# A hybrid HGRN2 / S5 / mixture-of-experts decoder step on one core: small matrix products laid side by side in the array, token columns split into equal halves, and the HGRN2 chunks issued ahead of their state

## What is computed

```
ada = silu(c) @ w_ada + b_ada             # 9 conditioning rows, 6 vectors of 1024 (+ 2 of w_ada_final)
proj = adanorm(x) @ w_in                  # q, f, i, g, u of 512 columns each
HGRN2 (4 heads, chunks of 32):  o = mask(q k) v + q S ;  S = decay * S + k v    # chunk after chunk
S5 (32 groups of 16 inputs, 64 complex states):  y = scan(u) ; y = glu(gelu(y))
x = x + gate1 * ([o | y] @ w_out)
x = x + gate2 * moe(adanorm(x))           # 4 groups x 8 experts, top 2 of the best group
y = adanorm_final(x)
```

## Time and profile before

| | us |
|---|---|
| runs shown (three) | 1017.25, 1021.3, 1029.67 |
| median | 1021.3 |
| the profiled execution | 1030.67 |
| its span, first to last instruction | 1028.7 |

### The profile page before, as it was taken

How to read it: one execution, slowest core, us unless ns; L and a number is a source line. 1 busy time by engine, 2 the same in 40 slices (tenths; PEclk the granted TensorE clock), 3 DMA queues, 4 the chain that set the end, 5 groups by cost and what they waited for, 6 DMA issues and landing times.

```text
span 1028.7 us, 8565 instructions
## 1 busy us (share of the span) xinstructions
PE 809.2 (79%) x3102; PEld 392.5 (38%) x3102; DVE 353.7 (34%) x905; ACT 208.3 (20%) x445; POOL 87.5 (9%) x134
## 2 busy tenths in 40 slices
PE   6189999999997999899679999934967787788800
PEld 1025566653353443777544442211422232233300
DVE  2029373546733234322523534340110101110157
ACT  2042123333344452100002101200110100110122
POOL 1000101120100001000001000032110101110040
PEclk9687999999998999555679999966988988898955
DMA  7940202024440106300159414553999999999552
GB/s 265 342 143 36 72 11 82 1 83 164 162 165 7 41 0 218 70 0 1 52 180 347 123 41 149 229 177 90 349 392 416 401 366 415 392 394 385 237 193 92
DMA packets 62844, 187.24 MB, mean 182 GB/s; under 512 B 12475, under 2 KB 17723, under 8 KB 50518
## 3 DMA queue, kind: packets, MB, share of 16 engines
q1 hardware_dynamic: 39542, 154.46, 39.5%
q10 hardware_dynamic: 16256, 17.04, 5.6%
q0 software_dynamic: 7008, 15.25, 4.6%
HBM read 176.84 MB, written 17.22 MB: 189 GB/s over the span
## 4 chain that ended last, share of the span: by engine, by line
PE 64%; DMA 15%; DVE 6%; ACTq 5%; issue 4%; ACT 3%; SPq 1%; POOL 1%; POOLq 0%; DVEq 0%
PE ps L1543 60%; DMA sb<-in_moe_w_up 12%; DVE sb L939 3%; PE ps L1595 2%; ACTq L613 2%; SPq L348 1%; ACTq L607 1%; PE ps L1690 1%; POOL token_of_row L507 1%; ACT sb L708 1%; DVE sb L1524 1%; DVE sb L1536 1%; DMA token_of_row<-sb 1%; DMA sb<-in_b_ada_final 1%; DMA sb<-y_rows,sb 1%
## 5 line engine op out<-in xcount | busy, mean ns | idle before, releaser
L1543 PE MATMUL ps<-sb 128*64 128x512 f32 (+10 forms) x2718 | 755.7, 508 | 106.5 <-DMA sb<-in_moe_w_up 51.3
L1543 PEld LDWEIGHTS ps<-sb 128*128 128x128 f32 (+4 forms) x2718 | 344.3, 174 | 485.7 <-issue 423.5
L939 DVE TENSOR_TENSOR sb<-sb 128x16 f32<-128x16 f32 (+18 forms) x368 | 162.6, 482 | 101.8 <-ACT sb L708 47.9
L939 DVE TENSOR_TENSOR sb<-ps,sb 128x256 f32<-128x256 f32 (+6 forms) x69 | 29.0, 441 | 238.3 <-ACT sb L885 188.4
L1595 PE MATMUL ps<-sb 128*128 128x128 f32 (+1 forms) x208 | 31.6, 302 | 35.4 <-DMA sb<-h_rows,sb 31.8
L1595 PEld LDWEIGHTS ps<-sb 128*128 128x128 f32 (+1 forms) x208 | 27.1, 197 | 52.4 <-DMA sb<-h_rows,sb 31.9
L885 ACT ACTIVATE sb<-ps 128x256 f32<-128x256 f32 x16 | 6.2, 385 | 177.0 <-PE ps L1543 177.0
L1246 DVE SCALAR_TENSOR_TENSOR sb<-sb,ps 128x128 f32<-128x128 f32 x60 | 16.8, 343 | 44.8 <-PE ps L1543 44.8
L515 POOL DMA_INDIRECT sb<-h_rows,sb x16 | 16.3, 1021 | 152.9 <-PE ps L1595 150.4
L708 ACT COPY sb<-ps 32x144 f32<-32x144 f32 x64 | 26.2, 410 | 11.1 <-PE ps L1543 9.6
L655 ACT ACTIVATE sb<-ps 128x512 f32<-128x512 f32 x12 | 7.2, 597 | 101.8 <-PE ps L1543 101.8
(11 more groups left out here) (229 smaller groups left out, 348.2 us busy)
## 6 DMA issues: line engine op xcount, KB each, us to landing
sb<-in_moe_w_gate SPq DMA_DIRECT2D x32, 1024.0 KB, 13.7
sb<-in_moe_w_up SPq DMA_DIRECT2D x32, 1024.0 KB, 16.1
sb<-in_moe_w_down SPq DMA_DIRECT2D x32, 1024.0 KB, 9.0
sb<-in_w_ada SPq DMA_DIRECT2D x12, 2048.0 KB, 8.8
sb<-in_w_in SPq DMA_DIRECT2D x5, 2048.0 KB, 9.3
sb<-in_w_ada_final SPq DMA_DIRECT2D x4, 2048.0 KB, 14.2
sb<-in_w_out SPq DMA_DIRECT2D x2, 2048.0 KB, 7.7
sb<-in_x_prompt SPq DMA_DIRECT2D x4, 512.0 KB, 10.9
```

The source lines that it names most:

```text
L939: return dve.tensor_tensor(out, x0, x1, op)
L1543: return pe.matmul(out, lhsT, rhs, start=start, stop=stop, skip_group_check=True)
```

## The change

1. Conditioning: the eight products of a piece go to four column groups of the array (PSUM partitions 0, 32, 64, 96; two products each, nine rows). ACT copies 105 rows of the bank to `part`, whose last rows hold the biases, and one product with a 0/1 matrix `pick` adds the four parts and the bias. For the first four pieces eight small products with `part` as the stationary side give columns at once, so that `ada_col` and its transposes go. A piece's bank is free for the piece after the next when its sum has been copied out.
2. The 576 columns are split 288 + 288 in `proj_cols`, the GLU and its sum of squares.
3. HGRN2: U products are issued for two chunks at a time, alternating between two row groups, into four banks, ahead of the state; the output products of a tile come after three of its four states, alternating between the four column groups; the transposes of a tile come one tile later; `Sr` has 8 buffers, in slot 0. On DVE the norm of a tile follows the state chain of the next one.
4. S5: the eight Toeplitz products go to four column groups of bank 6; ACT copies two of the four pairs, DVE the other two (8 copies each).

The core of the diff:

```
+        part = at(PART, 512)
+        pick = v2(take(16 * C9), 16, C9)
-        Sr = [v2(EXT + 2560 + 512 * k, H, P) for k in range(3)]
+        NSR = 8
+        Sr = [v2(512 * k, H, P) for k in range(NSR)]
+        ubank = [ps[6], ps[7], ps[0], ps[1]]
...
             # POOL
+            pool.memset(part, 0.0)
+            step(pool.memset(pick, 0.0))
+            for g in range(4):
+                step(pool.affine_select(out=pick, ...
...
             # ACT
+            def ada_parts(n):
+                act.wait_ge(S["ada_part"], n + 1)
+                if n >= 1:
+                    act.wait_ge(S["ada_sum"], n)
+                act.copy(part[0:PROWS, :], ada_bank(n)[0:PROWS, :]).then_inc(S["ada_pb"], 1)
...
+            for n_ in range(4):
+                ada_cols(n_)
+                if n_ + 1 < 4:
+                    ada_parts(n_ + 1)
...
-                        act.copy(Tm[32 * s:32 * s + 32, 2 * hf:2 * hf + 2, 32 * s:],
-                                 ps[6 + hf][0:32, :].rearrange("p (q n) -> p q n", q=2)[:, :, 0:w]).then_inc(S["s5_Tout"], 1)
+                        act.copy(Tm[32 * s:32 * s + 32, q, 32 * s:], ps[6][32 * q:32 * q + 32, 0:2 * P - 32 * s])\
+                            .then_inc(S["s5_Tout"], 1)
...
             # DVE
+                dve.wait_ge(S["s5_T"], 4 * (r + 1))
+                for q in (2, 3):
+                    for s in range(4):
+                        ins = dve.tensor_copy(Tm[32 * s:32 * s + 32, q, 32 * s:], ps[6][32 * q:32 * q + 32, 0:2 * P - 32 * s])
...
+            for t in range(PT):
+                state_chain(t)
+                if t >= 1:
+                    norm_o(t - 1)
                 if t + 1 < PT:
                     mask(t + 1)
-                norm_o(t)
+            norm_o(PT - 1)
...
             # PE
-                for c in range(KC):
-                    ins = mm(bank[q:q + C9, :], cT[:, c, :], w[:, c, :], c == 0, False)
-                j = 2 * v + h
-                mm(bank[q:q + C9, :], ident[0:16, j:j + 1].to_broadcast([16, C9]), bias16, False, True).then_inc(S["ada_mm"], 1)
+                if n >= 2:
+                    pe.wait_ge(S["ada_out"], n - 1)
+                for c in range(KC):
+                    g = 32 * (c % 4)
+                    ins = mm(bank[g:g + C9, :], cT[:, c, :], w[:, c, :], c < 4, c >= 4)
+                ins.then_inc(S["ada_part"], 1)
...
+                pe.wait_ge(S["ada_pb"], n + 1)
+                mm(ada_bank(n)[q:q + C9, :], pick[:, 2 * v + h, :], part, True, True).then_inc(S["ada_sum"], 1)
...
-                    mm(b0[:, :], lhs, hT[:, c, 0:TP], c == 0, c == KC - 1)
-                    ins = mm(b1[:, 0:NS], lhs, hT[:, c, TP:NT], c == 0, c == KC - 1)
+                    mm(b0[:, 0:NH], lhs, hT[:, c, 0:NH], c == 0, c == KC - 1)
+                    ins = mm(b1[:, 0:NH], lhs, hT[:, c, NH:NT], c == 0, c == KC - 1)
...
+                for k in range(2):
+                    for q in range(4):
+                        ins = mm(ps[6][32 * q:32 * q + 32, 0:256], AB[k][:, q, L - 1, :],
+                                 CA[k][:, q, 0:L, :].rearrange("p j h -> p (j h)"), k == 0, k == 1)
...
+            def chunk_pair(p):
+                if p >= 2:
+                    pe.wait_ge(S["s_upd"], 2 * (p - 1))
+                for h in range(H):
+                    hs = slice(P * h, P * (h + 1))
+                    for c in (2 * p, 2 * p + 1):
+                        js = slice(32 * (c % 4), 32 * (c % 4) + 32)
+                        ins = mm(ubank[c % 4][:, hs], KhT[js, c // 4, hs], V[js, c // 4, hs], True, True)
+                ins.then_inc(S["u_mm"], 1)
```

More of the change, by code:

```diff
@@ L168, in decoder_step @@
         iota_i = at(take(E), E)
+        yix, xix = (at(take(NU), NU) for _ in range(2))
+        roff = at(take(E), E)
         cb2 = v2(take(TILES * E), TILES, E)
@@ L299, in used_up @@
             if n < 4:
-                return S["ada_mm"], 2 + n + 1
+                return S["ada_part"], n + 1
             if n < 7:
@@ L849, in _ @@
                                     accum_out=RT["gs"][:, t:t + 1]))
-            for v, h in ADA_ROUTER[2:]:
-                late_row(v, h)
+            ada_parts(14)
+            ada_rows(14)
+            ada_parts(15)
+            ada_rows(15)
             act.wait_ge(S["rt_exp"], 2)
@@ L1233, in norm_o, with state_chain @@
                 ins.then_inc(S["o_norm"], 1)
-            mask(0)
-            for t in range(PT):
+            def state_chain(t):
                 for j in range(4):
                     c = 4 * t + j
-                    dve.wait_ge(S["u_mm"], c + 1)
-                    new, old, U = Sr[(c + 1) % 3], Sr[c % 3], ps[6 + c % 2].rearrange("p (h v) -> p h v", h=H)
+                    dve.wait_ge(S["u_mm"], c // 2 + 1)
+                    if j == 3 and t >= 1:
+                        dve.wait_ge(S["o_mm"], t)
+                    new, old, U = Sr[(c + 1) % NSR], Sr[c % NSR], ubank[c % 4].rearrange("p (h v) -> p h v", h=H)
                     if c == 0:
@@ new lines, in _, with ada_bank, ada_parts @@
+            pe.wait_ge(S["bc_out"], 1)
+            def ada_bank(n):
+                return ps[(2 if n >= 12 else 0) + n % 2]
+            def ada_parts(n):
+                bank, w = ada_bank(n), next_piece()
+                if n == 1:
+                    pe.wait_ge(S["bc_out"], 2)
+                if n >= 2:
[4 more added lines that the diff above has]
+                ins.then_inc(S["ada_part"], 1)
@@ L1673, in beside_s5 @@
                 for w in beside[j]:
-                    ada_row(*w) if j >= 4 else proj_cols(w)
+                    if j < 4:
+                        proj_cols(w)
+                        continue
+                    ada_parts(w)
+                    if w > 4:
+                        ada_sum_rows(w - 1)
             pe.wait_ge(S["const"], 1)
@@ L1751, in scores, with turn_out @@
                 ins.then_inc(S["sc_mm"], 1)
+            def chunk_pair(p):
[7 more added lines that the diff above has]
+                ins.then_inc(S["u_mm"], 1)
+            def turn_out(t):
+                r = ROWS[t]
+                pe.wait_ge(S["o_norm"], t + 1)
+                if t >= 1:
+                    pe.wait_ge(S["mix_out"], t)
+                for h in range(H):
+                    ins = pe.transpose(ps[3][:, P * h:P * h + r], mtok[t % 2][0:r, P * h:P * (h + 1)], ident[0:r, 0:r])
+                ins.then_inc(S["mix_tr"], 1)
             scores(0)
```

291 lines of the change are left out of this document (141 added, 150 removed).

## The result

The changed kernel takes 947.93 us (median of four runs, 945.03 to 951.06) against 1021.65 us before (four runs, 1017.25 to 1029.67): 0.927 of the time, 95% interval 0.921 to 0.934. The forecast was 930 us, the range 902 to 962. The profiled execution took 951.06 us.

What follows compares the result with a forecast made beforehand. The prediction took PE to bound the chain for 64% of the span and DMA, in the experts, for 15%. Its terms summed to 92.5 us off 1030.67, giving 938.2, scaled by 0.9% to 930 us; range 902 to 962.

Steps and rivals of the forecast that it cites:

- rival A: Products start strictly in written order, so four array groups work only in pairs; 958, scaled 949 us; chance 0.20.
- the units: Twelve projection units, split into equal halves: 7.8 us each, 0.85 less than 8.65; 10.2 us gained.
- the pieces and Toeplitz products: Four groups at once: a conditioning piece 7.72 to 1.75 us plus 0.87 sum; 16 Toeplitz instructions 3.45 to 1.05.
- the preparation: HGRN2 preparation: last head, the only one with conditioning, falls from 22.84 to 12.1 us; 9.7 gained.
- the way to the ranks: Router: the ranks begin near 657.4 instead of 673.4 us; 16 us gained in all.
- Rounds three and four: S5 rounds set by engines other than PE; 11.6 us gained less 5.6 for the clock, 6 kept.
- Four places can pay it; I charge 5.6: S5 rounds three and four: PE pauses before Toeplitz products and Y cost 2.4 us each for the clock's return.
- The sum of the chain, 33.5 a round: S5 rounds three and four: Y, copies, DVE work and scan add to 33.5 us a round against 39.3.
- Main part: HGRN2 main part: 10.4 us a tile on PE at half clock, 45.5 in all against 86; 43 gained.
- Moves earlier as a whole: Experts: the change does not shorten this stretch, near 269 us; gains before it move it earlier.
- I took 0.9% off: Whole kernel: 938.2 us scaled to 930, since the profiled execution was 0.9% above the median of 1021.3.
- Start: Start: conditioning ends near 73.5 instead of 75.65 us; 1.5 gained, ends 4 gained and 4 lost.

Runs made afterwards that it cites:

- e10: Changed kernel with the eight products of a conditioning piece written column group by column group instead of round the groups; 934.95 us (one run).
- e7: Changed kernel with unread PE products in S5 rounds three and four, and two conditioning copies moved ahead of ACT's third square; 929.74 us, ratio 0.907.
- e1: Changed kernel with unread PE products ahead of the first conditioning sum of S5 rounds three and four and before Y; 936.92 us, ratio 0.916.
- e9: As e7, with three unread products ahead of Y instead of six; 932.98 us, ratio 0.912.
- e3: Changed kernel with U and output products written chunk by chunk within their blocks, so neighbours share array rows or columns; 942.44 us, ratio 0.920.
- e6: Changed kernel with U products of the next tile issued behind this tile's output products instead of ahead; 949.19 us (one run).
- e8: Changed kernel with HGRN2 U, state wait and output products chunk by chunk as before the change; 968.07 us (one run).
- e11: Changed kernel with norm and transposes of a tile back in the same tile; 947.49 us (one run).
- the repeat: Changed kernel, unchanged, run again for a second profile and more times; 946.1 us, ratio 0.924.

## Why the prediction was right, and where it missed

**Right.** Direction, range and, outside the rounds and the main part, mechanism: four groups run side by side (rival A was wrong, e10), the units take 7.76, the pieces and Toeplitz products their forecast times, and the preparation, the GLU and the way to the ranks came within 1.1 us of their terms. The 2.4 us of the sample part were not forecast. The terms summed to 92.5; two profiles of each kernel give 83.6. That these are so close is in part luck: the main part gave 6.7 more than its term and the rounds 9.2 less.

**Rounds three and four: +6 forecast, -3.2 measured.** The step that failed is "Four places can pay it; I charge 5.6". The sum of the chain, 33.5 a round, was sound: in e7, with Y at full clock, the Y copies of two rounds are 36.9 us apart, some 2 of it overshoot. The price of the clock was the size that was off. I took 2.4 a place from a stretch of long dense products. Here half clock met W, Y and, through Y, ACT's copies, which came apart: 88.8 less 67 less 6.9 for the last copies is 14.9, not 5.6. The rows above account for 14 of it: 2.6 at W in round three, and in each round 3.2 for the first half of Y and 2.5 between the copies. e1, e7 and e9 show that this is the clock, by giving back 6.6, 8.0 and 4.3 us with only unread products added in the rounds.

**Main part: 43 forecast, 49.7 measured, by other reasons.** I computed PE's time at half clock, 10.4 a tile, with side-by-side products as its main saving. Now DVE sets the pace at 7 to 8 us a tile (my 7.3 for DVE was right), the clock is 0.81 to 0.88, and alternation is worth about 1 us (e3), issuing U ahead nothing (e6). What counts is one exchange between PE and DVE per tile instead of one per chunk (23, e8, with the products of a chunk in one group), the norm beside the next chain (7, e11) and the clock. What brought the clock stays open.

**Experts and ranks.** "Moves earlier as a whole" held in the repeat, 270.6 against 269.3 and 270.6. The first expert came 0.8 us less early than the ranks. The 16 us before the ranks did shorten the kernel.

**The median.** Unscaled, the forecast was 938.2 on the basis of the profiled execution; the changed kernel's two profiled executions lie 13 and 7 us above that (951.06 and 944.70). I took 0.9% off because the profiled execution of before was that far above the median, and that step failed: the second profiled execution of before took 1032.62, while its medians in three later sets of runs were 1022.6, 1026.2 and 1025.8 beside 1021.65, its single runs 1017 to 1038. The changed kernel scattered only from 945 to 951, with its profiled executions 3 above and 1 below their medians. So the excess of before had no counterpart after. Why before scatters more was not tried.

**Start.** 1.5 forecast, about 0 measured: from ACT's first copy to the first projection product 32.2 and 33.2 before, 31.8 and 33.1 after. The reason given, the column copy behind squares and root, was right: the third piece began at 60.14, as forecast, and e7 moved the copy and gained 2.9 to 4.2. What the sum had too small are the small products, put at 1.5 and twice 1.2:

```profile
52.32 2.09 PE L1582 MATMUL ps<-sb 128*64 128x9 f32 x16 [27.71 <-ACT sb L611]
...
72.68 2.09 PE L1582 MATMUL ps<-sb 128*64 128x9 f32 x16 [1.10 <-ACT sb L611]
```

## What to carry to other kernels

Saving PE work pays where PE is what is waited for; elsewhere the pauses that it leaves can cost the clock, and the next dependent products pay twice, as half of Y did here with 6 us instead of 3.1. So look, after such a saving, at the products just behind each new pause, and price them at half clock; some unread products ahead of a short dependent block were worth 8 us here. For a recurrence between two engines, count the exchanges per step first: putting four chunks into one exchange did more here (23 us) than the arrangement of the products in the array (1 us).

## What was not expected of the hardware

- Written order does not bind products of different groups even when the same group is written twice in a row (e10: 66 instructions in 7.26 us, as before in 7.28).
- A dense PE can be nearly as quick as a relieved one: e3 did 24% more busy time (29.95 against 24.13 us) in 5% more time, at a clock of 1.00 instead of 0.88.
- Nearly the same products in the main part ran at a granted clock of 0.53 before and 0.91 in e8, 57.97 and 34.47 us for 249 and 248 instructions.
